# The gates' projections moved inside the sliding-window attention of a two-block layer kernel

## The chip, the cores and the metric

The kernel runs on one core of one Trainium2 chip. The core has a matrix engine (TensorE, "PE" in the rows, with its weight loads "PEld"), a vector engine (VectorE, "DVE"), a scalar engine (ScalarE, "ACT"), a general engine (GpSimd, "POOL") and a queue that issues transfers (SyncE, "SP"). Each runs its own list of instructions in order, and they wait for each other by semaphores. The metric is the time of one execution on the device in microseconds; lower is better.

## The reference, cut to what matters

Two transformer-like blocks follow each other on 512 tokens of width 1024, in float32. Only the mixer of the first block is touched:

```
xn = rmsnorm(h, ln_mix_g)
z = xn @ w_in + b_in
q, k, v, pz, ga, gp = split(z, ...)      # widths 1024, 128, 128, 512, 1024, 1024
y_a = sliding_window_attention(q, k, v, sinks) @ w_attn_up
y_p = multiscale_pool(pz, w_pool_grp, pool_scale) @ w_pool_up
merged = sigmoid(ga) * y_a + sigmoid(gp) * y_p
h = h + merged @ w_o
...
# attention: 16 heads of 64 over 2 key/value heads; each block of 128 queries sees 256 keys,
# softmax with one extra "sink" logit for each head
# pool: running sums over windows of 2, 4, 8, 16 tokens, divided by counts, minus the input
```

The gates `ga` and `gp` are not needed before the two products `y_a` and `y_p` are multiplied by them.

## The kernel before

**Dense weights.** All large products use one stream of weight "slots". A slot is 128x1024 float32 numbers (512 KB): the weights of 128 output channels over all 1024 inputs, in 8 pieces of 128x128. For accuracy each product is three matmuls (`product`): high x high, high x low, low x high, where high is a value rounded to fp32r and low the rest. So a slot of a full product is 24 matmuls of 128x512. For each slot SP loads `weights_raw` (L141), ScalarE rounds it to `weights_high` (L150), GpSimd subtracts to get `weights_low` (L158). Raw, high and low each have two buffers. The rounding for slot j+2 waits until slot j has been used, the subtraction waits for the rounding, TensorE's slot j+2 waits for the subtraction. Results go to four accumulators in PSUM banks 0 to 3, each used again when its reader has signalled.

**Program order.** The kernel is cut into blocks; all engines meet at a barrier between two blocks. The first mixer has three of them.

1. *Projections* (`first_mixer`, first block): after the norm, 28 slots in seven turns of four: 8 for q, 8 for `ga`, 8 for `gp`, 4 for the pool input. ScalarE moves each result out of PSUM with its bias (L576), with Sigmoid for the gates. Then two slots for the keys, and one for v. The v slot is computed the other way round, so that tokens lie on partitions: 4 blocks of 128 tokens x 8 pieces x 3 = 96 matmuls of only 128 columns. VectorE adds its bias (L608).
2. *Attention* (`attention`): a hardware loop over the 4 blocks of 128 queries (`Fori`), with 8 steps unrolled in the body, each for two heads, 32 steps in all. At the head of a turn VectorE copies q and v of the block (L829, L831). A step is: scores on TensorE (L792), scale and mask (L837), row maximum (L842), negated maximum (L844) on VectorE, exponentials on ScalarE (L873, L875), sum, reciprocal, normalise on VectorE (L851, L853, L855), four transposes on TensorE (L805), copy out of PSUM on ScalarE (L882), product with the values on TensorE (L816), copy to the output on ScalarE (L886). The scores run two steps ahead of the transposes. GpSimd forms the window sums of the pool beside it (L772, L778, L781). No weights stream here.
3. *Gates and output* (`first_mixer`, last block): ScalarE and VectorE split the attention output in high and low (L383, L389); TensorE does four group products of the pool (L722), 8 slots of `w_attn_up`, 4 of `w_pool_up`, 8 of `w_o`. ScalarE scales the group products (L671), VectorE takes their low part (L691), then multiplies the finished accumulators by the gates (L695, L699) and adds (L704).

## Time and profile before

| what | value |
|---|---|
| median of 3 runs | 3261.18 us (3258.07 to 3262.68) |
| span of the profiled execution | 3257.4 us |
| TensorE busy | 2995.8 us (92%) |
| VectorE busy | 1793.6 us (55%) |
| ScalarE busy | 1068.2 us (33%) |
| GpSimd busy | 1265.8 us (39%) |
| mean granted TensorE clock | 0.964 |

The profile gives no other time for its execution than the span, 3.8 us under the median of the runs. TensorE is busy nearly everywhere; the first mixer is the exception: its first block lasts until about 214 us, its attention until 388.8 us, its last block until about 500 us.

### The profile page before, as it was taken

Reading aid. Unit: us, or ns where it says so; the run is one execution under the profiler, and the core shown is the slowest. Engines: PE = TensorE matmul, PEld = TensorE weight load, DVE = VectorE, ACT = ScalarE, POOL = GpSimd, SP = SyncE. Lnnn points to the kernel's source line nnn. Section 1 sums busy time; section 2 is a strip of 40 time slices with the busy share of each in tenths; the row PEclk is TensorE's granted clock in tenths of the full one; section 3 lists DMA queues with packets and bytes.
Section 4 is the critical chain, followed back from the end, with each engine's and each line's share of the span. In section 5 each row is a group of like instructions: output and inputs, shape, how many; then the busy total and the mean of one; then the engine's idle time right before and its main releaser. Section 6 shows DMA issues by size and latency. Waiting matters only on the chain. (4 is left out here: it accounts for less than half of the span.)

```text
span 3257.4 us, 52236 instructions
## 1 busy us (share of the span) xinstructions
PE 2995.8 (92%) x19808; PEld 2486.5 (76%) x19808; DVE 1793.6 (55%) x2626; ACT 1068.2 (33%) x1656; POOL 1265.8 (39%) x634
## 2 busy tenths in 40 slices
PE   7976698999999999999999999979869978899997
PEld 5864577888888888878888888856669966588775
DVE  1025426987477777427777777762836554433115
ACT  3324423333333333321111111134422335433323
POOL 3450033355444444444444444433332222244442
PEclk8988899999999999999999999989989989999998
DMA  3320022344445545565555555522652101233331
GB/s 119 97 71 0 7 85 90 92 141 141 126 163 205 175 159 174 211 185 190 197 196 196 196 190 190 184 91 78 205 150 52 36 15 39 65 96 96 98 104 65
DMA packets 173617, 404.59 MB, mean 124 GB/s; under 512 B 55216, under 2 KB 55344, under 8 KB 172208
## 3 DMA queue, kind: packets, MB, share of 16 engines
q1 hardware_dynamic: 173488, 402.72, 39.1%
q8 instruction: 100, 1.64, 0.2%
q14 instruction: 29, 0.24, 0.0%
HBM read 318.77 MB, written 83.89 MB: 124 GB/s over the span
## 5 line engine op out<-in xcount | busy, mean ns | idle before, releaser
L158 POOL TENSOR_TENSOR weights_low<-weights_raw,weights_high 128x1024 fp32r<-128x1024 f32 x435 | 1129.9, 2598 | 1686.6 <-ACT weights_high L150 1686.6
L150 ACT ACTIVATE weights_high<-weights_raw 128x1024 fp32r<-128x1024 f32 x435 | 461.0, 1060 | 1694.8 <-PE psum L258 1677.6
L256 PE MATMUL psum<-expert_in_high,weights_high 128*128 128x512 f32 x1152 | 458.4, 398 | 8.9 <-DVE expert_in_low L351 4.3
L257 PE MATMUL psum<-expert_in_low,weights_high 128*128 128x512 f32 x1152 | 449.7, 390 | 0.0
L258 PE MATMUL psum<-expert_in_high,weights_low 128*128 128x512 f32 x1152 | 449.6, 390 | 0.0
L256 PE MATMUL psum<-coefficients_high,weights_high 128*128 128x512 f32 x1024 | 399.6, 390 | 5.9 <-DVE coefficients_low L1172 4.2
L257 PE MATMUL psum<-coefficients_low,weights_high 128*128 128x512 f32 x1024 | 399.3, 390 | 0.0
L258 PE MATMUL psum<-coefficients_high,weights_low 128*128 128x512 f32 x1024 | 399.1, 390 | 0.0
L1172 DVE TENSOR_TENSOR coefficients_low<-activation_in,coefficients_high 128x512 fp32r<-128x512 f32 x128 | 354.8, 2772 | 4.4
L256 PEld LDWEIGHTS psum<-expert_in_high,weights_high 128*128 128x128 f32 x1152 | 217.1, 188 | 57.3 <-issue 10.2
L258 PEld LDWEIGHTS psum<-expert_in_high,weights_low 128*128 128x128 f32 x1152 | 216.8, 188 | 45.6
L257 PEld LDWEIGHTS psum<-expert_in_low,weights_high 128*128 128x128 f32 x1152 | 217.2, 189 | 41.3
L1153 DVE TENSOR_TENSOR second_key_weighted<-st_and_second_key_onehot,choices 128x512 f32<-128x512 f32 x128 | 225.7, 1763 | 19.4 <-DVE st_and_second_key_onehot L1149 2.2
L1169 DVE TENSOR_TENSOR coefficients_high<-activation_in,table_group 128x512 fp32r<-128x512 f32 x128 | 88.6, 692 | 264.6 <-PE psum L258 264.6
L256 PEld LDWEIGHTS psum<-coefficients_high,weights_high 128*128 128x128 f32 x1024 | 192.8, 188 | 46.7 <-DVE coefficients_low L1172 4.6
L258 PEld LDWEIGHTS psum<-coefficients_high,weights_low 128*128 128x128 f32 x1024 | 192.8, 188 | 40.2
L257 PEld LDWEIGHTS psum<-coefficients_low,weights_high 128*128 128x128 f32 x1024 | 192.8, 188 | 40.1
L1149 DVE TENSOR_TENSOR st_and_second_key_onehot<-tables,choices 128x1024 f32<-128x1024 f32 x128 | 157.1, 1227 | 115.1 <-PE psum L1050 100.5
L256 PE MATMUL psum<-mix_in_high,weights_high 128*128 128x512 f32 x464 | 187.3, 404 | 33.4 <-POOL weights_low L113 14.8
L257 PE MATMUL psum<-mix_in_low,weights_high 128*128 128x512 f32 x464 | 182.4, 393 | 0.0
L258 PE MATMUL psum<-mix_in_high,weights_low 128*128 128x512 f32 x464 | 182.2, 393 | 0.0
L256 PE MATMUL psum<-ffn_in_high,weights_high 128*128 128x512 f32 x352 | 138.3, 393 | 4.8 <-DVE ffn_in_low L351 4.8
(390 smaller groups left out, 4786.1 us busy)
## 6 DMA issues: line engine op xcount, KB each, us to landing
weights_raw<-in_weights SPq DMA_DIRECT2D x437, 512.0 KB, 3.6
expert_activations<-expert_activation SPq DMA_DIRECT2D x128, 256.0 KB, 4.2
coefficient_table<-table_stage SPq DMA_DIRECT2D x8, 4096.0 KB, 13.6
table_group<-coefficient_table SPq DMA_DIRECT2D x128, 256.0 KB, 4.1
activation_in<-expert_activations SPq DMA_DIRECT2D x128, 256.0 KB, 3.7
chunk_vectors<-scan_vectors SPq DMA_DIRECT2D x8, 1280.0 KB, 8.4
scan_vectors<-scan_stage SPq DMA_DIRECT2D x4, 1280.0 KB, 6.7
scan_vectors<-scan_stage SPq DMA_DIRECT2D x4, 1024.0 KB, 6.0
```

Source lines behind the costliest of these rows:

```text
L150: act.activation(d.hi[:, m % SPLIT, :], d.raw[:, m % RAW, :], ACT.Copy).then_inc(d.high, 1)
L158: pool.tensor_tensor(d.lo[:, m % SPLIT, :], d.raw[:, m % RAW, :], d.hi[:, m % SPLIT, :].bitcast(F32), ALU.subtract).then_inc(d.split, 1)
L256: pe.matmul(acc, w[0][:, cols], x[0], start=start, stop=False)
L257: pe.matmul(acc, w[0][:, cols], x[1], start=False, stop=False)
L258: return pe.matmul(acc, w[1][:, cols], x[0], start=False, stop=stop)
L1149: dve.tensor_tensor(onehot[:, u, :, :, :], iota[:, None, None, :].to_broadcast([P, 2, QT, NK]), sel[:, 0:2, bass.ds(t, QT)][:, :, :, None] ...
L1153: dve.tensor_tensor(second[:, u, :, :], onehot[:, u, 1, :, :], sel[:, 2, bass.ds(t, QT)][:, :, None].to_broadcast([P, QT, NK]), ALU.mult). ...
L1169: dve.tensor_tensor(by_block(co[0][:, o, :]), by_block(tile), gt, ALU.mult).then_inc(ex.part, 1)
L1172: dve.tensor_tensor(co[1][:, o, :], tile, co[0][:, o, :].bitcast(F32), ALU.subtract).then_inc(ex.coef, 1)
```

## The change

- The weight order becomes q, pool, keys, v, then `ga` and `gp`. The first block has 15 slots: three turns of four, two for keys, one for v.
- v is a slot like the others (24 matmuls of 128x512); ScalarE writes it with channels on partitions, TensorE turns it with four transposes, VectorE copies it in two pieces into a zeroed `values_by_token`.
- Attention is no longer a loop: its 32 steps are written out, read q and the values in place, and use PSUM banks 4 to 7. Between the scores and the value product of every step TensorE does half a gate slot (12 matmuls). After every second step ScalarE rounds the next weights and moves a finished gate slot out, with its bias but without Sigmoid; GpSimd takes the low parts between and after its pool work. The inverse counts lie in `gp`'s space.
- In the last block ScalarE applies Sigmoid to the eight chunks of `ga` after the rounding of the attention output, and to one chunk of `gp` after each of the eight slots; the scaling of pool group j comes after the rounding of weights that waits for slot j. VectorE's order is the same as before, with a wait for each gate.
- The mask has two block forms and not four.

```diff
@@ first_mixer, first block
             def _(pool):
-                pool.memset(vals[:, 0, :], 0.0).then_inc(zeroed, 1)
+                pool.memset(vals[:, :, :, :, :], 0.0).then_inc(zeroed, 1)
             def _(act):
                 gemm_out(lambda m: q[:, m, :], par("b_q"), ACT.Identity)
-                gemm_out(lambda m: ga[:, m, :], par("b_ga"), ACT.Sigmoid)
-                gemm_out(lambda m: gp[:, m, :], par("b_gp"), ACT.Sigmoid)
...
                 w.high(act, 0, NKV, 3)
+                w.full_wait(act, 0, NKV)
+                act.activation(vt[:, :], dense.acc[NKV], ACT.Identity, bias=par("b_v")).then_inc(dense.free[NKV], 1)
             def _(dve):
-                w.full_wait(dve, 0, 2)
-                dve.tensor_tensor(vals[:, 1:, :], dense.acc[2].rearrange("p (b n) -> p b n", b=NB),
-                                  par("b_v")[:, None, :].to_broadcast([P, NB, P]), ALU.add).then_inc(dense.free[2], 1)
+                dve.wait_ge(zeroed, 3)
+                dve.wait_ge(turned, 1)
+                for half in range(2):
+                    dve.tensor_copy(vals[:, 1:, :, half, half * HD:(half + 1) * HD],
+                                    ps[:, 5, :].rearrange("p (b v n) -> p b v n", b=NB, v=NKV))
             def _(pe):
-                w.multiply(pe, 7, lambda t: chunk(xn, t), [DC], lambda t: norm.ready(pe, t))
-                for v in range(NKV):
+                w.multiply(pe, 3, lambda t: chunk(xn, t), [DC], lambda t: norm.ready(pe, t))
+                for v in range(NKV + 1):
...
-                for b in range(NB):
-                    cols = slice(b * P, (b + 1) * P)
-                    for t in range(DC):
-                        x, y = chunk(xn, t, cols), (wv[0][:, t * P:(t + 1) * P], wv[1][:, t * P:(t + 1) * P])
-                        mm = product(pe, dense.acc[2][:, cols], x, 0, y, t == 0, t == DC - 1)
+                pe.wait_ge(dense.free[NKV], w.units // BANK + 2)
+                for b in range(NB):
+                    mm = pe.transpose(ps[:, 5, b * P:(b + 1) * P], vt[:, b * P:(b + 1) * P], consts("ident"))
@@ first_mixer, last block
             def _(act):
-                for g in range(G):
-                    act.wait_ge(group_done, g + 1)
-                    for dst in (yps, ypp[0]):
-                        ins = act.activation(dst[:, g, :], ps[:, 4 + g, :], ACT.Copy, scale=par("pool_scale")[:, g:g + 1])
-                    ins.then_inc(group_out, 1)
-                w.run(act, w.high, 2, BANK)
+                def gate(x, m):
+                    act.activation(x[:, m, :], x[:, m, :], ACT.Sigmoid).then_inc(gated, 1)
+                for m in range(DC):
+                    gate(ga, m)
+                for j in range(DC):
+                    w.high(act, 0, j, DC)
+                    if j < G:
+                        act.wait_ge(group_done, j + 1)
+                        for dst in (yps, ypp[0]):
+                            ins = act.activation(dst[:, j, :], ps[:, 4 + j, :], ACT.Copy, scale=par("pool_scale")[:, j:j + 1])
+                        ins.then_inc(group_out, 1)
+                    gate(gp, j)
             def _(dve):
                 for m in range(DC):
+                    dve.wait_ge(gated, m + 1)
                     w.full_wait(dve, m // BANK, m % BANK)
@@ attention
+    STEPS, GATES = NB * QC, 2 * DC
+    PART = DC * GATES // STEPS
             def _(pool):
...
+                w.low(pool, 0, 0, GATES)
                 pool.wait_ge(pooled, 6)
...
+                w.low(pool, 0, 1, GATES)
...
+                for j in range(2, GATES):
+                    w.low(pool, 0, j, GATES)
             def _(pe):
-                with pe.Fori(0, NB) as b:
-                    pe.wait_ge(staged, b * 3 + 3)
+                def gate_part(n):
+                    j, first = n * PART // DC, n * PART % DC
+                    if first == 0:
+                        w.free_wait(pe, j // BANK, j % BANK)
+                        w.slot_wait(pe, 0, j, GATES)
+                    for t in range(first, first + PART):
+                        mm = product(pe, dense.acc[j % BANK], w.weights(j), t, chunk(xn, t), t == 0, t == DC - 1)
+                    if first + PART == DC:
+                        mm.then_inc(dense.used, 1)
...
+                for n in range(STEPS):
+                    pe.wait_ge(probs, n + 1)
...  four transposes
+                    if n + 2 < STEPS:
+                        scores(n + 2)
+                    gate_part(n)
+                    pe.wait_ge(copied, n + 1)
+                    if n:
+                        pe.wait_ge(out, n)
...  four value products
             def _(act):
+                def gate_out(j):
+                    dst, bias = (ga, par("b_ga")) if j < DC else (gp, par("b_gp"))
+                    if j == DC:
+                        act.wait_ge(pooled, 6 + len(PW))
+                    w.high(act, 0, j, GATES)
+                    w.full_wait(act, j // BANK, j % BANK)
+                    act.activation(dst[:, j % DC, :], dense.acc[j % BANK], ACT.Identity,
+                                   bias=bias[:, j % DC:j % DC + 1]).then_inc(dense.free[j % BANK], 1)
```

TensorE, the middle of attention. One step of before, from its transposes (of `probabilities`) over the scores of two steps later to its value product:

```order
L805 MATMUL psum<-tables,probabilities 128x128 [waits transposed_copied,probs_ready]
L805 MATMUL psum<-tables,probabilities 128x128 x3
L792 MATMUL psum<-keys_by_kv_and_half,query_block 128x256 [waits scores_scaled]
L792 MATMUL psum<-keys_by_kv_and_half,query_block 128x256
L816 MATMUL psum<-probabilities_transposed,value_blocks 128x128 [waits attention_out,transposed_copied]
L816 MATMUL psum<-probabilities_transposed,value_blocks 128x128 x3
```

The same place now; the matmuls on `mix_in` are the gate part, three kinds, of which each comes four times in a step:

```order
L837 MATMUL psum<-tables,probabilities 128x128 [waits transposed_copied,probs_ready]
L837 MATMUL psum<-tables,probabilities 128x128 x3
L813 MATMUL psum<-keys_by_kv_and_half,q_then_attention_out 128x256 [waits scores_scaled]
L813 MATMUL psum<-keys_by_kv_and_half,q_then_attention_out 128x256
L256 MATMUL psum<-mix_in_high,weights_high 128x512
L257 MATMUL psum<-mix_in_low,weights_high 128x512
L258 MATMUL psum<-mix_in_high,weights_low 128x512
...
L849 MATMUL psum<-probabilities_transposed,values_by_token 128x128 [waits attention_out,transposed_copied]
L849 MATMUL psum<-probabilities_transposed,values_by_token 128x128 x3
```

Twelve matmuls of a gate slot stand between scores and value product where none stood; the waits of the attention's own matmuls are the same.

ScalarE, the start of the last block, before; `pool_in` and `pool_groups_split_high` are the scaled group products, a pair for each of four groups, all ahead of the first rounding of weights:

```order
L383 ACTIVATE tention_out_then_merged_high<-q_then_attention_out 128x512 x8
L671 ACTIVATE pool_in<-psum,params 128x512 [waits pool_group_product]
L671 ACTIVATE pool_groups_split_high<-psum,params 128x512
...
L164 ISA
L149 ISA [waits weights_loaded1]
L150 ACTIVATE weights_high<-weights_raw 128x1024 [waits weights_used]
```

And now; the last four rows come four times in a row, once for each group:

```order
L383 ACTIVATE tention_out_then_merged_high<-q_then_attention_out 128x512 x8
L666 ACT_TABLE_LOAD
L666 ACTIVATE gate_attention<-gate_attention 128x512 x8
L150 ACTIVATE weights_high<-weights_raw 128x1024 [waits weights_used,weights_loaded1]
L675 ACTIVATE pool_in<-psum,params 128x512 [waits pool_group_product]
L675 ACTIVATE pool_groups_split_high<-psum,params 128x512
L666 ACTIVATE gate_pool<-gate_pool 128x512
```

Each group's scaling now stands behind a rounding of weights, the fourth group's behind the fourth rounding, which waits until slot 3 has been used. On VectorE the low parts of all four groups (L691 before, L696 now) still stand ahead of the first product with a gate (L695, now L701), which frees the accumulator of slot 0.

## Rows read from the trace of the kernel before

**Rows 1.** The page, the span in 40 slices: busy tenths of TensorE

```profile
PE   7976698999999999999999999979869978899997
```

**Rows 2.** Windows: us, busy of PE, PEld, DVE, ACT, POOL, clock, DMA, GB/s

```profile
36.00:199.00 163.00, 163.00 (x716) 134.80 (x716) 0.00 (x0) 53.47 (x63) 69.46 (x29) 0.99 0.32 100
214.00:388.80 174.80, 103.41 (x512) 82.95 (x513) 92.42 (x205) 77.13 (x261) 22.04 (x15) 0.80 0.03 9
388.80:459.00 70.20, 69.00 (x296) 55.47 (x296) 18.05 (x28) 21.59 (x28) 26.34 (x11) 1.00 0.25 82
```

**Rows 3.** Timeline of ScalarE around v: start, us, operation [idle before <- releaser]

```profile
193.78 1.06 ACT L150 ACTIVATE weights_high<-weights_raw 128x1024 fp32r<-128x1024 f32 x1 [3.81 <-PE psum L258]
199.22 1.06 ACT L150 ACTIVATE weights_high<-weights_raw 128x1024 fp32r<-128x1024 f32 x1 [3.11 <-PE psum L258]
209.89 1.06 ACT L150 ACTIVATE weights_high<-weights_raw 128x1024 fp32r<-128x1024 f32 x1 [8.21 <-PE psum L258]
```

**Rows 4.** Timeline from the end of the first block to attention's first transposes

```profile
211.02 2.34 POOL L158 TENSOR_TENSOR weights_low<-weights_raw,weights_high 128x1024 fp32r<-128x1024 f32 x1 [8.29 <-ACT weights_high L150]
214.13 0.95 POOL L764 MEMSET value_blocks<- 128x1024 f32 x1 [0.77 <-POOLq L533]
214.26 1.28 ACT L873 ACT_TABLE_LOAD   x1 [3.32 <-PEq L533]
215.34 4.15 POOL L772 TENSOR_TENSOR window_sums_a<-pool_in 128x2048 f32<-128x2048 f32 x1
219.98 3.78 PE L792 MATMUL psum<-keys_by_kv_and_half,query_block 128*128 x8 [10.19 <-DVE value_blocks L831]
222.22 0.69 DVE L837 SCALAR_TENSOR_TENSOR scores<-psum,mask_by_block 128x512 f32<-128x512 f32 x1 [2.38 <-PE psum L792]
228.92 1.11 PE L805 MATMUL psum<-tables,probabilities 128*128 128x128 f32 x4 [5.16 <-DVE probabilities L855]
```

**Rows 5.** Timeline of a step in the middle of a turn, and who waited in attention

```profile
245.22 0.66 PE L805 MATMUL psum<-tables,probabilities 128*128 128x128 f32 x4 [1.75 <-DVE probabilities L855]
245.72 1.03 PE L792 MATMUL psum<-keys_by_kv_and_half,query_block 128*128 x4
246.58 1.14 PE L816 MATMUL psum<-probabilities_transposed,value_blocks 128*128 128x128 f32 x8
246.78 0.69 DVE L837 SCALAR_TENSOR_TENSOR scores<-psum,mask_by_block 128x512 f32<-128x512 f32 x1 [1.62 <-PE psum L792]
249.47 0.66 PE L805 MATMUL psum<-tables,probabilities 128*128 128x128 f32 x4 [1.74 <-DVE probabilities L855]
PE psum L805 <- DVE probabilities L855: 53.6, 28, 5.2
```

**Rows 6.** Timeline of VectorE beside GpSimd; min/median/max ns of L704

```profile
227.05 1.26 POOL L778 TENSOR_TENSOR pooled<-window_sums_b,inverse_counts 128x512 f32<-128x512 f32 x1
227.34 1.52 DVE L855 TENSOR_TENSOR probabilities<-probabilities,reciprocal 128x512 f32<-128x512 f32 x1
L704 DVE TENSOR_TENSOR gate_attention<-gate_attention,gate_pool x8: 677/682/2656, 459.3 to 469.2; 128x512 f32<-128x512 f32 x8
```

**Rows 7.** Timeline of the last block's first slot

```profile
388.78 4.27 ACT L383 ACTIVATE ion_out_then_merged_high<-q_then_attention_out 128x512 fp32r<-128x512 f32 x8 [0.54 <-PEq L756]
391.91 0.79 PE L256 MATMUL psum<-ion_out_then_merged_high,weights_high 128*128 128x512 f32 x1
396.94 0.72 ACT L671 ACTIVATE pool_groups_split_high<-psum,params 128x512 fp32r<-128x512 f32 x1
397.70 0.69 DVE L691 TENSOR_TENSOR pool_groups_split_low<-pool_in,pool_groups_split_high 128x512 fp32r<-128x512 f32 x1 [0.47 <-ACT pool_groups_split_high L671]
398.00 1.06 ACT L150 ACTIVATE weights_high<-weights_raw 128x1024 fp32r<-128x1024 f32 x1 [0.33 <-PE psum L258]
```

**Rows 8.** TensorE after an idle stretch: timeline row, and the window that follows

```profile
463.45 0.76 PE L256 MATMUL psum<-ion_out_then_merged_high,weights_high 128*128 128x512 f32 x1 [5.65 <-DVE tion_out_then_merged_low L389]
463.50:467.90 4.40, 4.40 (x11) 3.35 (x12) 4.40 (x8) 2.25 (x4) 0.00 (x0) 0.50 0.16 64
```

More of the change, by code:

```diff
@@ L551, in _ @@
                 pool.memset(keys[:, :, :, :], 0.0).then_inc(zeroed, 1)
[L552 removed]
+                pool.memset(vals[:, :, :, :, :], 0.0).then_inc(zeroed, 1)
                 pool.memset(zp[:, :, 0:16], 0.0).then_inc(zeroed, 1)
                 dense.low_first(pool)
[L555 removed]
+                w.run(pool, w.low, 3, BANK)
                 w.run(pool, w.low, 1, 3)
@@ new lines, in _, with scores @@
+                w = dense.cursor()
+                def scores(n):
+                    c = n % QC
+                    if n >= 2:
+                        pe.wait_ge(scaled, n - 1)
+                    for half in range(2):
+                        mm = pe.matmul(score_bank(n)[:, half * 2 * P:(half + 1) * 2 * P], q[:, c, block_of(n)],
+                                       keys[:, c * NKV // QC, half, n // QC * P:n // QC * P + 2 * P], start=True, stop=True)
+                    mm.then_inc(scored, 1)
@@ new lines, in _, with exp @@
+                w = dense.cursor()
+                def exp(n):
+                    act.wait_ge(negmax, n + 1)
+                    for half in range(2):
+                        j, head = 2 * n + half, n % QC * 2 + half
+                        act.activation(e[:, n % 2, half, :], s[:, n % 2, half, :], ACT.Exp, bias=nm[:, j:j + 1],
+                                       accum_out=su[:, j:j + 1]).then_inc(exps, 1)
+                        act.activation(es[:, j:j + 1], par("sinks")[:, head:head + 1], ACT.Exp,
+                                       bias=nm[:, j:j + 1]).then_inc(exps, 1)
@@ new lines, in _ @@
+                exp(0)
+                exp(1)
+                for n in range(STEPS):
+                    act.wait_ge(turned, n + 1)
+                    act.activation(pt[:, :], ps[:, TURNED, :], ACT.Copy).then_inc(copied, 1)
+                    if n + 2 < STEPS:
+                        exp(n + 2)
+                    if (n + 1) * PART % DC == 0:
+                        gate_out((n + 1) * PART // DC - 1)
+                    act.wait_ge(mixed, n + 1)
+                    act.activation(q[:, n % QC, block_of(n)], ps[:, OUT, 0:P], ACT.Copy).then_inc(out, 1)
```

208 lines of the change are left out of this document (86 added, 122 removed).

## The prediction

> **What bounds the kernel now.** I read first the 40 slices of the page: TensorE is busy nine tenths or more almost everywhere, but six or seven tenths in slices 3 to 5 [rows 1]. The stretches of the first mixer then show why [rows 2]. From 36 to 199 us TensorE is busy 163 of 163 us: the projections are bound by it, so a slot taken away there is worth its whole length. From 214 to 388.8 us it is busy 103.4 of 174.8 us at a mean granted clock of 0.80: attention is bound by a chain, not by an engine. From 388.8 to 459 us it is full again. The waits name the chain [rows 5]: TensorE's transposes waited 53.6 us in 28 places for VectorE's normalised probabilities. One step is 4.25 us (245.22 to 249.47): transposes, scores of two steps later, VectorE from 246.78 (scale, maximum, normalise), transposes again. Of it TensorE needs only what lies from 245.22 to about 247.6. So gate slots put into the rest are hidden until TensorE itself is full; the question is what a step costs then.
>
> **Taken from the first block.** ScalarE's rounding starts right after each slot, so its starts are the slots' pitch: 199.22 - 193.78 = 5.44 us a slot, 24 matmuls at 0.227 [rows 3]. Sixteen gate slots are 87.0 us. The v slot took 209.89 - 199.22 = 10.67 us and becomes a normal one: 5.2 us less. Its new tail (ScalarE copy, four transposes, two VectorE copies) lies beside the last rounding and GpSimd's 2.34 us subtraction, which held the barrier before too: attention begins 4.24 us after that rounding (209.89 to 214.13) [rows 3, 4], and about 4.6 after TensorE was done, since a rounding starts some 0.4 us behind the slot that it waits for (the drain of the last matmul and a semaphore, my estimate from matmul rows longer than their pitch). I take 0 for the tail; it ends about when the subtraction does, and would cost up to 0.5 us.
>
> **A step of attention.** TensorE per step at full clock, start to start: transposes 245.22 to 245.72, 0.50; scores to 246.58, 0.86; value product, eight passes in 1.14 us of which the last is about 0.28 long, so 0.98; gate part 12 x 0.227 = 2.72 [rows 5]. Sum 5.06 us. The chain needs 4.25, so TensorE has 0.8 us to spare for it and becomes the bound. Does ScalarE or GpSimd spoil that? ScalarE gets a 1.06 us rounding and a copy out of PSUM of 0.7 us every second step, after the gate part; it then is about 1.3 us late with the next copy of transposes, which TensorE asks for only behind the next gate part. The weights of the following slot have had two steps (10.1 us) to be made. So 32 x 5.06 less two steps without scores (1.7) = 160.2 us.
>
> **Attention's start.** Staging of q and v is gone, so the scores start at once, but at the low clock (3.78 us for eight passes, as before), and the first transposes came 8.94 us after the scores (219.98 to 228.92) [rows 4]. Here the window sums of GpSimd lie right beside it, and they hold VectorE up: the normalise took 1.52 us when it began inside a 1.26 us GpSimd operation and ended 0.55 after it, and L704, with two SBUF operands, took up to 2.66 us against 0.68, as if behind a whole subtraction of 2.34 [rows 4, 6]. L837, with a PSUM operand, kept 0.69 beside the window sums [rows 4]. Going through the negated maxima, the sum and the normalise with window sums of 4.15 us for four groups and, in proportion, 3.1, 2.1 and 1.0 for three, two and one, each holding one of them up, the transposes start at 11.7 us; bounds 8.9 (no hold-up) and 14.8 (as before, 228.92 - 214.13).
>
> **Clock and hold-ups inside.** The first 4.4 us after a long idle run at half speed: after 5.65 us of idle, the window 463.5 to 467.9 has 0.50 [rows 8]. That costs 2.2 us here. Two more places have GpSimd back to back: the first two subtractions are each followed by four pool operations of about 1.3 us, in steps 2 and 4. Three VectorE operations in a step want in between; I get 1.6 us late for TensorE in each, 3.2 together (bounds 0 and 6). The other subtractions end about when the negated maximum wants to start, inside the 0.8 to spare.
>
> The Trainium skill (Advanced Engine Details and Errata, Mode Summary) says that GpSimd blocks Vector instructions of the two-port modes, and a float32 tensor_tensor is none of these. By that the hold-ups would be nothing here. Rows 6 say otherwise, and I go by them; the skill's GPSIMD Engine Reference, Specifications, adds two SBUF inputs to the list.
>
> **Attention's end.** After the last gate part come a rounding, a subtraction and the barrier, the same 4.6 us as above; the value product covers 0.98 of it: 3.6 us. Attention is 11.7 + 160.2 + 2.2 + 3.2 + 3.6 = 180.9, against 388.77 - 214.13 = 174.6: +6.3 us. That is what carrying 87 us of gates costs it.
>
> **The last block gets a new stall.** Before, the four groups were scaled and split by 398.4 while TensorE was in its first slots [rows 7]. Now the fourth scaling stands behind the rounding that waits for slot 3, at 398.00 + 3 x 5.44 = 414.32. Rounding to 415.4; two scalings of about 0.6 to 416.5; then the low part L696, which has two SBUF operands and meets the 2.34 us subtraction of GpSimd from about 415.5 to 417.9: it ends at 418.5; the product with the gate (L701) ends at 419.1 and frees the accumulator of slot 0, for which TensorE's slot 4 has waited since 413.9 (0.4 ahead of the rounding). That is 5.2 us (4.1 without the meeting), and after it the clock is likely low for 4.4 us as in rows 8: +2.2, bounds 0 and 2.2. Behind TensorE in that stall nothing else is late; slots 5 to 7 find VectorE caught up, and the packed pool slots begin 20 us later. The eight Sigmoids with a table load of 1.28 us [rows 4] put the first rounding at 388.8 + 4.2 + 1.3 + 8 x 0.53 = 398.6 instead of 398.0: slot 2 is wanted at 403.1 and its subtraction ends at 402.1, so nothing. The group products may start at the low clock since TensorE idles 3.6 us before them: the clock held through the 1.75 us waits of rows 5 (transposes 0.66 us long, and 1.11 at the low clock in rows 4) and fell behind 5.65; 3.6 is midway, and I take 1.1, bounds 0 and 2.2. Block: +8.5 us.
>
> **Sum.** -87.0 - 5.2 + 6.3 + 8.5 = -77.4 us. Span 3257.4 - 77.4 = 3180.0; the median of the runs stood 3.8 over the profile's span, so 3183.8: I say 3184. Everything behind the first mixer is the same work in the same order, shifted.
>
> **Rivals.**
>
> A. *The small costs are mostly not paid.* GpSimd loses the race for the port, the clock does not fall in the stall: 1.1 + 2.2 + 1.1 in the last block, 3.2 in steps 2 and 4, 1.4 at the start: 9 us less, 3175. For it: all four are bounds of mine and no row is of this very place. Against: rows 6 and 8.
>
> B. *TensorE is not the bound of a step.* If the chain cannot run under the gate part, the step goes towards 4.25 + 2.72 = 6.97 us, 32 times 1.9 more, at most +61. That needs TensorE's place in the order to delay the scores, but they stand ahead of the gate part. Partly, it can come through a hold-up of VectorE by the fourteen later subtractions: 2.34 us each, of which 0.8 is free, 14 x 1.5 = +21: 3205. The timing I work out puts them where only single-operand work runs; a shift of 1 us would change it.
>
> C. *Slower than before.* The granted clock goes low through attention, where it was 0.80 on average. At half speed a step takes 10.1 us and attention 162 more: 3346. It decides from a step of 5.06 + 77.4/32 = 7.5 us on, a mean clock of about 0.67. For it: that 0.80. Against: the steps of rows 5 held the full clock with 1.75 us idle in each, and the projections, full, held 0.99 [rows 2].
>
> The Trainium skill (TensorE: Matmul & The Clock Gate, "A second HAM failure mode: psum-queue depth-cycling") describes a kernel that goes through PSUM banks with short idles between groups and whose clock swings for that. This change cycles through six banks in each step; by that rule C would hold. No row here shows such swings without long idles.
>
> **Chances and range.** Forecast 58%, A 22%, B 16%, C 3%, and 1% that something unseen leaves no difference. The measurement cannot tell less than about 0.2% (6.5 us) from no change. The range takes A's whole effect with 3 more below, and most of B above: 3172 to 3203. Faster 0.96, same 0.01, slower 0.03.
>
> **What would show it.** In the profile after: attention without a loop, its transposes 5.06 us apart in the middle with clock 1.00 and TensorE full; the slot pitch before it unchanged and 15 slots; first transposes 9 to 12 us after the barrier; a single TensorE idle of 4 to 5.5 us before the fifth slot of the last block, released by VectorE's L701, and half clock behind it. Steps over 5.5 us apart with TensorE idle would prove me wrong for B, steps that long with it full for C. No idle before the fifth slot would mean that I misread VectorE's order.

## The result and the profile after

The changed kernel takes 3174.59 us (median of 4 runs, 3171.35 to 3180.6) against 3260.64 us of the kernel before on the same chip (4 runs, 3258.07 to 3262.68). The ratio is 0.9735, with a 95% interval of 0.972 to 0.9749. Five more runs in a later measurement gave 3173.07 us (3168.95 to 3176.22), ratio 0.9728 (0.9715 to 0.9742). The forecast was 3184 us with 3172 to 3203 as its range: the time lies inside it, 9 us under the forecast.

The profiled execution has a span of 3170.1 us and a mean granted TensorE clock of 0.971. Two views answer to [rows 1, 2]: TensorE's row of the page (its busy tenths in 40 slices), and windows of the first mixer. A window row gives its start and end in us, its length, the busy time of PE, PEld, DVE, ACT and POOL with their numbers of instructions, the granted clock, the DMA share and the GB/s moved.

```profile
PE   7899889999999999999999999979699977999997
```

```profile
32.00:120.40 88.40, 84.66 (x364) 69.37 (x364) 1.29 (x2) 26.14 (x32) 38.31 (x17) 0.96 0.32 101
120.40:129.70 9.30, 3.75 (x8) 2.52 (x8) 7.11 (x10) 2.93 (x12) 8.97 (x6) 0.68 0.43 169
129.70:134.00 4.30, 4.29 (x12) 3.60 (x13) 1.38 (x2) 0.60 (x1) 1.08 (x1) 0.50 0.02 4
140.00:290.00 150.00, 148.89 (x847) 130.79 (x845) 74.92 (x176) 89.81 (x267) 47.33 (x24) 1.00 0.18 53
324.00:329.40 5.40, 4.87 (x12) 3.83 (x13) 2.09 (x4) 0.00 (x0) 0.00 (x0) 0.50 0.36 97
329.40:360.00 30.60, 30.60 (x136) 25.34 (x135) 4.09 (x7) 7.44 (x10) 12.00 (x5) 1.00 0.26 77
```

The slices that showed six or seven tenths now show eight or nine. TensorE was busy 103.4 of the attention's 174.8 us at a clock of 0.80; with the gates in it the attention's middle has 148.9 of 150 at 1.00, and the whole of it (120.4 to 292.6) 162.9 of 172.2 at 0.97. Counted in the two profiles, in us:

| stretch | forecast | measured |
|---|---|---|
| first matmul to start of attention | -92.2 | -92.4 (180.7 to 88.2) |
| attention | +6.3 (180.9) | -2.4 (174.6 to 172.2) |
| last block | +8.5 | +9.1 |
| before the first matmul | 0 | -1.3 |
| all that follows | 0 | about 0 (offset -87.0 at the mixer's end, -87.3 at the kernel's) |

**A step.** TensorE's timeline in the middle of the attention (start, us, operation), with all gate matmuls but the first of the step left out, answers to [rows 5]:

```profile
187.21 0.60 PE L837 MATMUL psum<-tables,probabilities 128*128 128x128 f32 x4
187.64 1.03 PE L813 MATMUL psum<-keys_by_kv_and_half,q_then_attention_out 128*128 128x256 f32 x4
188.32 0.58 PE L256 MATMUL psum<-mix_in_high,weights_high 128*128 128x512 f32 x1
...
191.24 1.05 PE L849 MATMUL psum<-probabilities_transposed,values_by_token 128*128 128x128 f32 x8
192.13 0.60 PE L837 MATMUL psum<-tables,probabilities 128*128 128x128 f32 x4
```

The transposes come 4.92 to 4.93 us apart and no row has an idle time: the next piece always starts before the end of the one ahead of it. The wait that stood first in [rows 5], 53.6 us for the probabilities, has fallen to this (the waits from 140 to 290 us: in total, times, longest):

```profile
PE psum L837 <- DVE probabilities L879: 0.3, 1, 0.3
```

**The start.** From the first scores to the second transposes: TensorE, and the two VectorE operations that took longer than elsewhere with the GpSimd window sums beside them. They answer to [rows 4, 6]:

```profile
120.45 3.75 PE L813 MATMUL psum<-keys_by_kv_and_half,q_then_attention_out 128*128 128x256 f32 x8 [1.70 <-PEq L534]
124.39 2.75 POOL L789 TENSOR_TENSOR window_sums_b<-window_sums_a 128x1536 f32<-128x1536 f32 x1
125.69 1.47 DVE L869 SCALAR_TENSOR_TENSOR negated_max<-row_max,negated_sinks 128x2 f32<-128x2 f32 x1
127.21 1.90 POOL L789 TENSOR_TENSOR window_sums_a<-window_sums_b 128x1024 f32<-128x1024 f32 x1
127.45 2.20 DVE L879 TENSOR_TENSOR probabilities<-probabilities,reciprocal 128x512 f32<-128x512 f32 x1
129.71 1.12 PE L837 MATMUL psum<-tables,probabilities 128*128 128x128 f32 x4 [5.51 <-DVE probabilities L879]
130.62 1.92 PE L813 MATMUL psum<-keys_by_kv_and_half,q_then_attention_out 128*128 128x256 f32 x4
137.28 0.60 PE L837 MATMUL psum<-tables,probabilities 128*128 128x128 f32 x4
```

The first transposes come 129.71 - 120.45 = 9.26 us after the first scores. The first step takes 137.28 - 129.71 = 7.57 us where the later ones take 4.93: the window 129.7 to 134 above shows half clock with TensorE full.

**The end.** From the last value products to the last block:

```profile
288.12 1.05 PE L849 MATMUL psum<-probabilities_transposed,values_by_token 128*128 128x128 f32 x8
289.35 0.67 ACT L908 ACTIVATE gate_pool<-psum,params 128x512 f32<-128x512 f32 x1
289.52 2.34 POOL L158 TENSOR_TENSOR weights_low<-weights_raw,weights_high 128x1024 fp32r<-128x1024 f32 x1 [5.59 <-ACT weights_high L150]
292.66 5.10 PE L729 MATMUL psum<-pooled,pool_group_weights 128*128 128x512 f32 x8 [3.48 <-PEq L771]
```

TensorE stands idle for 3.48 us; the forecast said 3.6. What the barrier waits for is not attention's own output but the making of a later slot: ScalarE's rounding, then GpSimd's subtraction to 291.86, then SyncE's issue of a load at 291.88.

**The last block.** ScalarE's roundings, and the stall they frame; they answer to [rows 7, 8]:

```profile
314.23 1.06 ACT L150 ACTIVATE weights_high<-weights_raw 128x1024 fp32r<-128x1024 f32 x1 [2.70 <-PE psum L258]
319.67 1.06 ACT L150 ACTIVATE weights_high<-weights_raw 128x1024 fp32r<-128x1024 f32 x1 [2.70 <-PE psum L258]
320.80 2.35 POOL L158 TENSOR_TENSOR weights_low<-weights_raw,weights_high 128x1024 fp32r<-128x1024 f32 x1 [3.03 <-ACT weights_high L150]
321.91 1.78 DVE L696 TENSOR_TENSOR pool_groups_split_low<-pool_in,pool_groups_split_high 128x512 fp32r<-128x512 f32 x1 [3.59 <-ACT pool_groups_split_high L675]
323.62 2.47 DVE L701 TENSOR_TENSOR gate_attention<-psum,gate_attention 128x512 f32<-128x512 f32 x4
324.54 0.77 PE L256 MATMUL psum<-ion_out_then_merged_high,weights_high 128*128 128x512 f32 x1 [4.97 <-DVE gate_attention L701]
332.75 1.06 ACT L150 ACTIVATE weights_high<-weights_raw 128x1024 fp32r<-128x1024 f32 x1 [10.36 <-PE psum L258]
```

The pitch of the slots is 5.44 us up to the fourth (319.67 - 314.23); the next takes 332.75 - 319.67 = 13.08: 7.6 more. Of it 4.97 is the idle time released by VectorE's L701, and the rest is the half clock to 329.4: the window 324 to 329.4 above has 0.50 for 5.4 us, which costs 2.7.

### The profile page after: what moved, and what is told of

Read it like the earlier page. It is cut to its first block and busy times, and to the rows that moved or that the text cites. A ratio compares the mean times of both kernels' runs of the same rounds, so it can differ in the third digit from the quotient of the medians.

```text
span 3170.1 us, 51665 instructions
## 1 busy us (share of the span) xinstructions
PE 2966.9 (94%) x19740; PEld 2471.1 (78%) x19740; DVE 1791.9 (57%) x2615; ACT 1067.1 (34%) x1666; POOL 1265.8 (40%) x633
## 5 line engine op out<-in xcount | busy, mean ns | idle before, releaser
L256 PE MATMUL psum<-mix_in_high,weights_high 128*128 128x512 f32 x472 | 197.0, 417 | 32.8 <-POOL weights_low L113 14.8
```

The source lines that it names most:

```text
L256: pe.matmul(acc, w[0][:, cols], x[0], start=start, stop=False)
```

## The experiments

The reasons under test are: that TensorE's own queue is the bound of a step (against: only the engine's total load, or the chain and the gates in a row); that the start, the end and the last block's fifth slot cost what the forecast said, by the mechanism it said; and what each part of the change is worth alone. The kernel before was run beside each of them, with medians from 3258.6 to 3260.0 us; the ratios are to these. The code of the edits is shortened, in places to words.

### Only the attention unrolled, gates where they were

```
-                    gate_part(n)                  # and its copies out, roundings and loads
+  gates back in the first block's loops, sigmoid in their copy out as before
```

> The kernel after, but with the 16 gate slots (and Sigmoid) back in the first block; attention is unrolled and holds no gate work, and the last block is that of before. It tells what unrolling is worth by itself. My theory: a step is the chain's 4.25 us all the way, start 9.3 us as in the kernel after, no turn edges, so attention takes 9.3 + 30 x 4.25 + about 6 for the last two steps and the end = 143 us against 174.6, 32 less; with v 5.2 less: 3260.6 - 37 = 3224, and the gates' own share of the 86 us is then about 49. Rival (the edges of the loop cost nothing much, the gain is all the gates' hiding): 3255, and the gates' share 80.

Measured: 3226.57 us (3220.0 to 3228.95), ratio 0.9896 (0.9877 to 0.9914). A step:

```profile
252.51 0.66 PE L822 MATMUL psum<-tables,probabilities 128*128 128x128 f32 x4 [1.72 <-DVE probabilities L863]
253.00 1.03 PE L798 MATMUL psum<-keys_by_kv_and_half,q_then_attention_out 128*128 128x256 f32 x4
256.73 0.66 PE L822 MATMUL psum<-tables,probabilities 128*128 128x128 f32 x4 [1.72 <-DVE probabilities L863]
```

4.22 us a step with 1.72 idle, the chain of [rows 5] unchanged. The unrolling with the v slot is worth 32 us by itself against the kernel run beside it (3258.6). In the profiles its attention is 29.3 us shorter (174.6 to 145.3): in the loop the last transposes of a turn and the first of the next were 12.1 to 12.2 us apart, at three places, where this kernel has 4.22, which makes 24; and its first transposes come 9.26 us after the barrier in place of 14.8. The gates' move is worth the other 52 (3226.6 to 3174.6). That is 87 us taken out of the first block less about 27 that attention grows by (145.3 us from 209.68 to the block behind it at 354.94, and 172.2 with gates) and 8 in the last block.

### The gate part ahead of the next scores

```
+                    gate_part(n)
                     if n + 2 < STEPS:
                         scores(n + 2)
-                    gate_part(n)
```

> The kernel after with one swap in TensorE's order: the half gate slot stands ahead of the scores and not behind them. The same work and the same matmuls. My theory (the chain from transposes over scores and VectorE to the next transposes is hidden only because the scores stand first): the step becomes 4.25 + 2.7 to 2.9 = 7.0 to 7.2 us against 4.93, 30 times 2.1 to 2.2 more: about 3174.6 + 64 = 3239, TensorE idle about 2 us in each step. Rival (TensorE's full load sets the step whatever the order): no change, 3175.

Measured: 3241.42 us (3240.43 to 3241.68), ratio 0.9944 (0.9929 to 0.9959). The instructions are the same, with one pair exchanged, and 67 us of the gain go:

```profile
255.89 0.66 PE L837 MATMUL psum<-tables,probabilities 128*128 128x128 f32 x4 [1.81 <-DVE probabilities L879]
...
259.14 1.02 PE L813 MATMUL psum<-keys_by_kv_and_half,q_then_attention_out 128*128 128x256 f32 x4
262.86 0.66 PE L837 MATMUL psum<-tables,probabilities 128*128 128x128 f32 x4 [1.80 <-DVE probabilities L879]
```

6.97 us a step, the 4.25 + 2.72 of rival B, with TensorE idle 1.8 us in each. What the gates' move gains hangs on the place of the scores in TensorE's queue: with the gates ahead of them the kernel is 15 us slower than with the gates left in the first block (3226.6).

### A whole slot in every second step

```
                 def gate_part(n):
-                    j, first = n * PART // DC, n * PART % DC
+                    if n % 2:
+                        return
+                    PART = DC
+                    j, first = n // 2, 0
```

> The same 192 products, but a whole slot of 24 in every second step in place of 12 in each. Theory (what a step costs is the longer of TensorE's queue in it and the chain from the transposes to the next probabilities, 4.22 us with nothing in between as the kernel without gates in the attention shows): a step with a slot takes 4.93 + 12 x 0.227 = 7.65, one without it 4.22, so 11.87 for two where the changed kernel has 9.86: 16 x 2.0 = 32 us more, 3207. Rival (only the engine's total work counts, since scores run two steps ahead and even the load out): no change, 3174.6.

Measured: 3204.95 us (3201.44 to 3208.68), 2 us off the 3207. Three transposes:

```profile
153.97 0.60 PE L840 MATMUL psum<-tables,probabilities 128*128 128x128 f32 x4
...
158.14 0.65 PE L840 MATMUL psum<-tables,probabilities 128*128 128x128 f32 x4 [1.72 <-DVE probabilities L882]
...
165.88 0.60 PE L840 MATMUL psum<-tables,probabilities 128*128 128x128 f32 x4
```

4.17 us without a slot and 7.74 with one, 11.9 for two against 9.86. The scores run two steps ahead, but TensorE takes its queue in order and each step waits for VectorE's probabilities (1.72 us idle in a step without a slot): time that one step leaves idle is not made good in the next. The rival (only total load counts) is out.

### The gate part one step ahead

```
                 scores(1)
+                gate_part(0)
...
-                    gate_part(n)
+                    if n + 1 < STEPS:
+                        gate_part(n + 1)
```

> The 12 gate products of step n are queued one step earlier, those of the first step before the first transposes. Theory (TensorE is the bound of the attention, and what it does while the first chain of steps is still coming costs nothing): the first step falls from the 7.57 us that the changed kernel shows to the 4.93 us of the later ones, 2.6 less, and the last 12 products move from the last step, where the chain through copy and products with v is what the end waits for, for about 1.3 more: some 4 us less than the changed kernel's 3174.6, 3170.6. Rival (the first step's length is the chain's own, through VectorE's maximum and ScalarE's exponential of the next step, and the end waits for the last step's chain as before): no change, 3174.6. Second rival: the first products of the first slot wait for its rounding and delay the first transposes by as much as they save: no change either, with the first transposes later than 129.7.

Measured: 3168.14 us (3166.43 to 3169.87), ratio 0.9715 (0.9703 to 0.9728): 5 to 6.5 us less than the changed kernel, more than expected. Start and end:

```profile
131.91 0.66 PE L838 MATMUL psum<-tables,probabilities 128*128 128x128 f32 x4 [2.12 <-DVE probabilities L881]
136.91 0.60 PE L838 MATMUL psum<-tables,probabilities 128*128 128x128 f32 x4
...
285.02 2.35 POOL L158 TENSOR_TENSOR weights_low<-weights_raw,weights_high 128x1024 fp32r<-128x1024 f32 x1 [6.43 <-ACT weights_high L150]
286.23 1.16 PE L851 MATMUL psum<-probabilities_transposed,values_by_token 128*128 128x128 f32 x8 [1.11 <-ACT probabilities_transposed L917]
288.18 5.29 PE L729 MATMUL psum<-pooled,pool_group_weights 128*128 128x512 f32 x8 [0.79 <-PEq L771]
```

The first step takes 5.00 us, not 7.57: the low clock (0.71 on average from 120.0 to 131.9) runs out in time that TensorE had to spare anyway; from 131.9 to 136.9 it is 1.00. Both rivals fall: the first transposes come 9.27 us after the first scores, as before the edit (9.26). At the end, from the last transposes (284.51) to the next block is 3.7 us where it was 7.7 (284.91 to 292.66). I had expected 1.3 of those 4. The moved products account for 1.5 (3.21 to 1.72 us from the last transposes to the value product). The rest is the chain named above: the last rounding starts 0.6 us before the last transposes (283.88) where it started 3.5 us behind them (288.38), and TensorE's idle time at the barrier falls from 3.48 to 0.79. So the mechanism that the forecast gave for the end (rounding, subtraction, barrier) is shown, by starting it earlier.

### The groups' scaling ahead of the sigmoids

```
-                for m in range(DC):
-                    gate(ga, m)
+                for g in range(G):
+                    ... wait for group g, scale it twice
                 for j in range(DC):
                     w.high(act, 0, j, DC)
-                    if j < G:
-                        ... wait for group j, scale it twice
+                    gate(ga, j)
                     gate(gp, j)
```

> The kernel after, with ScalarE's order in the last block changed: the four pool groups are scaled at once after the rounding of the attention output, and one Sigmoid of each gate follows each slot. My theory (the 5 us stall ahead of the fifth slot, and the low clock behind it, come from the fourth group's scaling behind the fourth rounding): no stall, 7.6 us less, 3167. Rival (the stall comes from the Sigmoids or VectorE's backlog anyway): under 2 us less, 3173 or more, and the stall stays in the profile.

Measured: 3166.73 us (3166.28 to 3171.33), ratio 0.972 (0.9706 to 0.9733), 6 to 8 us less than the changed kernel. The stall is gone, and the half clock with it. The edit also spreads the Sigmoids of `ga` over the slots; that the scaling was what VectorE waited for is read from the changed kernel's rows (L696 released by ScalarE's `pool_groups_split_high`):

```profile
320.87 1.06 ACT L150 ACTIVATE weights_high<-weights_raw 128x1024 fp32r<-128x1024 f32 x1 [3.34 <-PE psum L258]
322.48 0.69 DVE L700 TENSOR_TENSOR gate_attention<-psum,gate_attention 128x512 f32<-128x512 f32 x1 [4.75 <-ACT gate_attention L666]
```

```profile
305.00:330.00 25.00, 25.00 (x112) 20.71 (x111) 3.46 (x5) 11.45 (x16) 12.02 (x5) 1.00 0.27 84
```

### Both mends, and then GpSimd's sums out of the start

The two edits above in one kernel:

> The two mends together: the scaling of the groups' products ahead of the gates' sigmoids (alone 3166.7), and the gates' products queued one step earlier. They act at different places, the last block's first slot and the attention's two ends, so their gains add: 3166.7 - 4 = 3163. If the gate products ahead bring nothing alone, they bring nothing here: 3166.7. If the later stages take gains of this size back, as they did with the v slot alone, 3165 to 3168 with the first mixer 4 us shorter all the same.

Measured: 3161.51 us (3157.06 to 3162.19), ratio 0.9691 (0.9679 to 0.9704). The gains add: 11.6 to 13.1 us together, 11.3 to 14.3 one by one. In this kernel the first transposes still wait for VectorE, which is held beside the window sums as in the changed kernel:

```profile
126.18 1.47 DVE L870 SCALAR_TENSOR_TENSOR negated_max<-row_max,negated_sinks 128x2 f32<-128x2 f32 x1
127.95 2.20 DVE L880 TENSOR_TENSOR probabilities<-probabilities,reciprocal 128x512 f32<-128x512 f32 x1
130.21 0.66 PE L837 MATMUL psum<-tables,probabilities 128*128 128x128 f32 x4 [2.40 <-DVE probabilities L880]
```

The next kernel cuts the first window sum in two and gives each of GpSimd's then thirteen operations on the pool branch a step to wait for, from the second step on:

```
+                    pool.wait_ge(probs, at[-1])    # 2, 3, 5, 6, 7 for the sums, 8 to 11 products, 12 to 15 differences
```

> The kernel with both mends (3161.5), with GpSimd's 4 window sums, 4 products and 4 differences each held until VectorE has made the probabilities of a named step, so that they run in the 2.3 us in which VectorE waits for the next scores, and none before the first transposes; the first sum is cut in two. Theory (VectorE's 1.47 and 2.20 us operations at the start of the attention are 0.16 to 0.35 and 0.69 us operations held up by GpSimd's sums): the first transposes come 2.4 us earlier, 6.9 in place of 9.3 us after the start, until TensorE's first 12 gate products, which end 2.4 us before them now, are the bound; later steps lose at most 0.5: 3159. Rival (the holds are not GpSimd's doing, or the first step's start is set by the half clock of the first 8 score products alone): 3161.5, with VectorE's operations as long as before.

Measured: 3157.44 us (3154.17 to 3159.14), ratio 0.9689 (0.9676 to 0.9702). Its median is 4 us lower and the lowest of all, but the two ranges of runs overlap and so do the ratios' intervals; what the edit did is shown by the profile:

```profile
124.38 0.16 DVE L877 SCALAR_TENSOR_TENSOR negated_max<-row_max,negated_sinks 128x2 f32<-128x2 f32 x1
124.84 0.69 DVE L887 TENSOR_TENSOR probabilities<-probabilities,reciprocal 128x512 f32<-128x512 f32 x1
126.02 0.60 PE L844 MATMUL psum<-tables,probabilities 128*128 128x128 f32 x4
```

1.47 became 0.16 and 2.20 became 0.69. The first transposes come 6.2 us after the first scores (119.78 to 126.02), not 9.3, and TensorE is busy without a pause until them (6.20 of 6.20 us): its own queue is the bound there too, from the first scores on. The steps behind them are 4.92 to 4.94 us apart from the first on, where the changed kernel has 5.00, 5.38 and 5.01 for its fourth to sixth. The holds are GpSimd's doing; the rival is out. A smaller part came by itself: the low clock of the start ended earlier in this profile, and the first eight score products took 3.11 us and not 3.75.

### v: alone, alone and later, and taken back

```
-  96 products of 128 columns with x stationary, VectorE adds the bias
+  24 products of 512 columns, ScalarE adds the bias, 4 transposes, VectorE copies
```

> The kernel before, with the new v slot alone: 24 wide matmuls, copy, four transposes, one copy, and the gates and the attention loop as before. My theory: the slot shrinks from 10.67 to 5.44 us and its tail ends no later than the last subtraction of GpSimd, so 5.2 us less than before: 3255.4. Rival (the tail of copies and transposes holds the barrier): 1 to 2 us of it given back, 3257. The profile tells them apart by what ends last ahead of the barrier.

Measured: 3261.57 us (11 runs, 3253.88 to 3266.24), ratio 1.0008 (0.9999 to 1.0018). No gain. Yet in its profile attention starts at 207.4 instead of 214.1 us and the first mixer ends 7.0 us earlier. The rival, that the tail of copies and transposes holds the barrier, is out: VectorE's copy ends at 206.41, GpSimd's last subtraction at 206.68. The lead shrinks in stages that nothing touched: it is 5.4 us at 860 us and 2.1 at 2780, and at the end the kernel is 0.6 behind. One place where some of it goes is the window from 2445 to 2470 us (granted clock 0.93 and 1.00; the v slot's kernel first, the kernel before second):

```profile
2445.00:2470.00 25.00, 23.27 (x648) 22.38 (x644) 15.10 (x34) 5.86 (x15) 9.31 (x12) 0.93 0.29 56
```

```profile
2445.00:2470.00 25.00, 24.45 (x748) 23.82 (x750) 14.10 (x34) 6.79 (x17) 9.08 (x12) 1.00 0.30 56
```

Was it the hour at which later stages meet such a dip of the clock? The next kernel puts everything about as late as before the v slot:

```
+        for n in range(5):
+            act.activation(self.hi[:, 0, :], self.raw[:, 0, :], ACT.Copy)...   # ahead of the first rounding
```

> The kernel of the v slot alone, with five more roundings of the first weights on ScalarE ahead of the first (each 1.06 us, their results written over), so that the first block and everything behind it comes 5.3 us later than in that kernel, and at about the hour of the kernel before. Theory (the 7.0 us that the v slot gains by the end of the first mixer were lost later to the hour at which unchanged stages meet the clock's throttle): the later stages meet it as in the kernel before and the loss is not there: the 5.3 us are not paid, 3258 to 3262. Rival (the loss belongs to the kernel with the v slot itself, whatever the hour): the delay is paid in full, 3261.6 + 5.3 = 3266.9. Third: a delay ahead of the first matmul is itself hidden behind the load of x and the first norm, and everything stays at 3261.6 with no shift of the first block; then the run says nothing.

Measured: 3265.91 us (12 runs, 3262.46 to 3272.96), ratio 1.002 (1.0011 to 1.0028). First matmul at 39.04 instead of 32.85. Against the kernel of the v slot 4.3 us are paid of the 5.4 that the five roundings take: by the medians the delay is paid nearly in full, the rival holds, and the theory of the hour falls. (The profiled execution was the slowest of the twelve, so its stages are not used.)

The other way round, the changed kernel with v as it was (the lines with - above in place of those with +):

> The changed kernel with v alone as it was: its 96 products of 128 columns with x as the stationary operand in the first block's last slot, and the two halves written by VectorE with the bias added. Theory (the v slot's gain is real, and that the kernel with nothing but the v slot did not keep it is that kernel's own affair): the 5.2 us that the sum gave to v come back, 3174.6 + 5 = 3180, and the attention starts some 5 to 7 us later. Rival (a gain of that size in the first mixer is always lost in the later stages, as it was alone): 3174.6, with the attention starting later all the same.

Measured: 3183.56 us (3181.96 to 3184.52), ratio 0.9767 (0.9754 to 0.9781): 9 to 10.5 us more than the changed kernel. In the profiles the first mixer ends 5.8 us later, of which 0.6 lie ahead of the first matmul, so 5.2, the term of the sum to a tenth. Another 2.5 come by 770 us and 3.4 by 2820, again in stages that the edit does not touch. So the v slot's 5.2 us are real in the first mixer in both pairs; behind it, unchanged stages have taken it all back in one pair and nearly doubled it in the other, by medians of 4 to 15 runs. What decides that is open.

And the changed kernel itself, with no edit:

> The changed kernel itself once more, to have more runs to measure the others against (its four so far lie between 3171.4 and 3180.6, wider than the others'). If the 3174.6 holds, v as before costs 9 and the two mends bring 13; if it is nearer to the profiled 3172.2, v costs 11 and they bring 10.7. If it is nearer to 3178, v costs the 5 of the sum.

Measured: 3173.07 us (3168.95 to 3176.22), between the first two cases. Its profiled execution has a span of 3174.2 us against the 3170.1 of the first, with no edit between them: 1.0 lies ahead of the first matmul and 2.7 more have come by 2650 us. So of what single profiles show in stages behind the first mixer, about 3 us is the scatter of one kernel; v's worth in the whole is 9 to 10.5 us and the two mends' 11.6 to 13.

## Why the prediction was right, and where it was 9 us high

**The bound and its change: right.** The chain before, TensorE's queue after; the step without gates keeps 4.22 us, with gates TensorE is full at clock 1.00, and gates ahead of the scores restore the chain at 6.97.

**The first block: right.** -92.2 against -92.4, with the pitch of 5.44 us. The tail costs 0.2 us in this profile: VectorE's second copy ends at 120.14, behind GpSimd's subtraction (117.13 to 119.47), and attention starts at 120.41, which is 0.94 us behind the subtraction where it was 0.77. The forecast had 0 to 0.5.

**A step: 5.06 forecast, 4.93 measured; 4 of the 9 us.** The mis-sized term is the sum of start-to-start times, which I took at the loop's pieces. Between those start times lay short waits. Transposes 0.50 are 0.43, value products 0.98 are 0.89, and scores 0.86 are 0.68: in the loop the weight loads of the value product waited for ScalarE's copy at 27 places, 12.3 us in all. The gate part errs the other way, 2.92 in place of 2.72 (188.32 to 191.24; its first matmul stands 0.42 us ahead of the next, the others 0.23). So the 0.13 is about what is left of 0.34 too much and 0.20 too little; 31 times it is 4.0. A piece that follows an idle time was also longer ([rows 5] show transposes of 0.66 us with 1.75 idle in front; the rows after show 0.60 with none).

**The start: 11.7 forecast, 9.3 measured; 2.4 us.** The mechanism was right, as the run with the sums moved shows. The size was not: sums of 3.60, 2.75, 1.90 and 1.60 us hold two VectorE operations for 1.3 and 1.5 us and a third for 0.2 (0.35 in place of 0.16), where I had one held by each sum and began with 4.15.

**Hold-ups in steps 2 and 4: 3.2 forecast, 0.6 measured; 2.6 us.** VectorE is held there as well (the normalise takes 1.48 and 1.47 us, 0.69 otherwise), but the step's slack of 0.8 us, now measured as 4.93 - 4.22 = 0.7, takes most of it. I had charged the hold-up where only what goes past the slack is paid.

**Low clock at the start: 2.2 forecast, 2.6 measured. The end: 3.6 and 3.5.** Right, and by the mechanisms given; the gate part one step ahead takes away the first, and 2.7 of the second.

**The sum.** In spans the forecast is 9.9 us high (3180.0 against 3170.1): 8.7 from the attention, the rest from 1.3 that came ahead of the first matmul, where nothing was changed, and from small terms. The median stands 4.5 us over the span and not 3.8, which makes it 9. The three larger misses lie on the same side, so none of them hid another.

**The last block: +8.5 forecast, +9.1 measured.** The fifth slot is late by 4.97 + the half clock = 7.6 (7.4 forecast), released by L701, with L696 lengthened to 1.78 us by the subtraction beside it, each as said. The scaling moved ahead takes it away. The group products take 1.4 more after 3.48 us of idle (5.10 against 3.67), not 1.1: the clock from 292.6 to 296 is 0.57, which costs 1.5.

**The rivals.** A (3175) has the number by luck, and not the reason. Of its costs that would not be paid, three were: the half clock in the stall, the subtraction beside L696, and the low clock at the group products, 4.4 us together. Two were not: the hold-ups in steps 2 and 4, and the 1.4 at the start. Another 4 us come from the length of a step, of which A says nothing. B did not occur, and its condition is now shown from both sides. Its second way, through the later subtractions, is in the trace but stays inside the slack: beside one of them the negated maximum takes 0.58 us in place of 0.16, and the steps stay at 4.93:

```profile
165.52 0.58 DVE L869 SCALAR_TENSOR_TENSOR negated_max<-row_max,negated_sinks 128x2 f32<-128x2 f32 x1
```

C did not occur: the clock rose, 0.80 to 1.00. The Trainium skill (TensorE: Matmul & The Clock Gate, "A second HAM failure mode: psum-queue depth-cycling") tells of a kernel whose clock swings as it goes through PSUM banks with short idles between groups. The window from 140 to 290 us shows 1.00, but there the pauses are gone. (A step here writes four banks, for the transposes, the scores, the gate slot and the output; the six of the prediction are a miscount.) The nearer cases have the pauses. The kernel without gates in the attention is idle for 1.72 us in every step of 4.22, with three banks in each, and its clock is 1.00 from 232 to 350 us. The kernel before has the same steps, and there the clock did fall again, at the beginning of two turns: 0.58 from 236.6 to 240.0 and 0.57 from 274.0 to 277.5 us, behind idles of 2.4 and 2.7 us. So the prediction's "no row here shows such swings without long idles" does not hold for the whole trace; what sets these stretches off from the even ones is not shown. On VectorE beside GpSimd the Trainium skill's GPSIMD Engine Reference, Specifications, names contention also for instructions with two SBUF inputs. The trace agrees: 1.47 us fell to 0.16 and 2.20 to 0.69. The Trainium skill's Advanced Engine Details and Errata, Mode Summary, names the two-port modes alone, and these rows are a case that it leaves out.

**Everything behind the first mixer as before: right for this pair (-87.0 and -87.3), not in general,** as the v slot's runs show: there 4 us or more came or went. That it held so closely here is partly luck, since a second profile of the changed kernel differs by 3 us behind the first mixer.

## What to carry to other kernels

Independent matmuls put into a chain's idle time cost nothing in this kernel only until the engine's in-order queue in that one step is full; they belong behind what feeds the chain, in equal parts, and one step ahead so that they fill the start and leave the end. Price a hold-up only by what goes past the slack of its step. After moving work, follow what was queued behind it on every engine: here 16 to 17 us more (3173.1 or 3174.6 to 3157.4) came from a gate part, a scaling and the window sums that stood in the wrong place of their queues.

## What the runs showed of the hardware

- GpSimd holds up VectorE operations with two SBUF operands however small: one that writes 128x2 elements took 1.47 us beside a window sum and 0.16 without. Operations with an operand in PSUM (L862, the scaling of the scores) kept 0.69 us beside a GpSimd subtraction of 2.39.
- A short idle does not decide whether the clock falls. After 3.48 us of idle TensorE ran its next 3.4 us at a mean clock of 0.57. With the gate part one step ahead it ran 3.5 us at 0.52 behind two idles of 1.11 and 0.79 us; the kernel with the sums moved has the same two idles (1.11 and 0.79) at the same place and kept 1.00. In this order:

```profile
288.10:291.60 3.50, 3.42 (x5) 1.53 (x6) 2.78 (x5) 3.44 (x7) 0.00 (x0) 0.52 0.49 152
281.50:285.00 3.50, 3.41 (x9) 1.63 (x9) 2.77 (x5) 3.43 (x7) 0.00 (x0) 1.00 0.56 154
```

  The kernel before had 0.96 us of idle there and 1.00 for the eight group products, but 0.55 from 383.4 to 386.6, over its last transposes. The 1.72 us in every step of the kernel without gates left the clock at 1.00 from 232 to 350 us. What brings the low clock at a given place is open.
- A gain of 5 us in one stage of this kernel cannot be counted on in its time: by the medians unchanged stages took 8 us with the v slot alone and gave 4 to 5 with it in the changed kernel, and two executions of one kernel differed by 3 us there.
